# Branch products that wait for each head block, two gathered pairs added ahead of the sums, and one root per tile in the last norm

## What is computed

```python
for l in range(2):
    h = rms(x, norm1_g) * (1 + sc1) + sh1
    qa, ..., ga, gs, gr = split(h @ w_in)            # heads of three branches, three gates
    z = (sigmoid(ga) * (o_na @ w_br_na) + sigmoid(gs) * (o_swa @ w_br_swa)
         + sigmoid(gr) * (o_ret @ w_br_ret))         # the branch products
    x = x + g1 * (z @ w_out)
    h2 = rms(x, norm2_g) * (1 + sc2) + sh2
    x = x + g2 * experts(h2)                         # sum of each token's two expert rows
y = rms(x, final_norm_g)
# rms(x, g) = x * rsqrt(mean(x * x) + 1e-6) * g
```

## Time and profile before

| what | us |
|---|---|
| median of 3 timed runs | 1163.63 (1163.27 to 1164.51) |
| the profiled execution, its own time | 1159.58 |
| its span, from first to last instruction | 1157.8 |
| TensorE busy in the span | 1078.5 |
| VectorE busy | 689.8 |
| ScalarE busy | 440.6 |
| GpSimd busy | 197.0 |

### The profile page before, as it was taken

One profiled execution on the slowest core, in us unless ns is written; L12 is line 12 of the kernel. 1 busy time (PEld: TensorE's weight loads), 2 busy tenths in 40 slices (PEclk: granted clock), 3 DMA queues, 4 the chain that ended last, 5 costly groups with the idle time before them and its releaser, 6 DMA issues.

```text
span 1157.8 us, 23661 instructions
## 1 busy us (share of the span) xinstructions
PE 1078.5 (93%) x9845; PEld 895.0 (77%) x9845; DVE 689.8 (60%) x1477; ACT 440.6 (38%) x946; POOL 197.0 (17%) x224
## 2 busy tenths in 40 slices
PE   4999999999999989999879999999999998999995
PEld 2667778889897678888657677888998885888883
DVE  3535565645476657776663335655455858577667
ACT  4442245543423423332342232655234333333332
POOL 0021140000020123222211111300000301332313
PEclk9999999999999999999989999999999999999998
DMA  9988897223336699999846998421242467799985
GB/s 324 348 234 223 233 340 247 74 79 103 115 110 254 210 370 364 360 373 372 318 152 201 246 221 247 144 63 48 80 143 95 127 252 273 265 357 364 366 309 186
DMA packets 136335, 265.96 MB, mean 230 GB/s; under 512 B 9846, under 2 KB 91926, under 8 KB 128032
## 3 DMA queue, kind: packets, MB, share of 16 engines
q1 hardware_dynamic: 119280, 220.18, 55.6%
q0 software_dynamic: 16192, 42.06, 12.8%
q10 hardware_dynamic: 752, 2.15, 0.5%
HBM read 248.71 MB, written 26.74 MB: 238 GB/s over the span
## 4 chain that ended last, share of the span: by engine, by line
PE 78%; DVE 9%; DMA 6%; ACT 3%; issue 2%; POOL 1%; SPq 0%; DVEq 0%; POOLq 0%; ACTq 0%
PE ps L1036 17%; PE ps L827 16%; PE ps L1244 13%; PE ps L1285 6%; PE ps L1156 6%; PE ps L1171 5%; DMA arena<-in_ada_w 3%; PE ps L749 2%; DMA ring<-in_w_in 2%; PE ps L1234 2%; DMA arena<-scratch_xs,token_i 2%; PE ps L980 2%; PE ps L1020 2%; PE ps L1002 2%; PE ps L1323 1%
## 5 line engine op out<-in xcount | busy, mean ns | idle before, releaser
L627 DVE TENSOR_TENSOR w_lo<-ring,w_hi 128x512 fp32r<-128x512 f32 x128 | 87.7, 690 | 132.2 <-ACT w_hi L617 132.0
L617 ACT ACTIVATE w_hi<-ring 128x512 fp32r<-128x512 f32 x128 | 80.3, 631 | 209.8 <-PE ps L827 145.6
L624 DVE TENSOR_TENSOR w_lo<-ring,w_hi 128x512 fp32r<-128x512 f32 x128 | 88.1, 689 | 109.3 <-ACT w_hi L615 109.3
L1036 PE MATMUL ps<-h_hi,w_hi 128*128 128x384 f32 x384 | 133.8, 348 | 4.7 <-ACT arena L2452 4.7
L615 ACT ACTIVATE w_hi<-ring 128x512 fp32r<-128x512 f32 x128 | 80.3, 629 | 148.7 <-PE ps L1036 103.3
L1036 PE MATMUL ps<-h_hi,w_lo 128*128 128x384 f32 x384 | 128.7, 335 | 0.0
L1036 PE MATMUL ps<-h_lo,w_hi 128*128 128x384 f32 x384 | 128.7, 335 | 0.0
L827 PE MATMUL ps<-w_hi,h_hi 128*128 128x512 f32 x288 | 116.1, 403 | 5.0 <-issue 2.6
L827 PE MATMUL ps<-w_hi,h_lo 128*128 128x512 f32 x288 | 113.1, 393 | 0.0
L827 PE MATMUL ps<-w_lo,h_hi 128*128 128x512 f32 x288 | 113.0, 392 | 0.0
L1244 PEld LDWEIGHTS ps<-arena,ring 128*64 128x64 f32 x1920 | 80.2, 137 | 7.8 <-issue 7.8
(11 more groups left out here) (347 smaller groups left out, 2189.7 us busy)
## 6 DMA issues: line engine op xcount, KB each, us to landing
ring<-in_w_in SPq DMA_DIRECT2D x48, 1024.0 KB, 5.4
ring<-in_ada_w SPq DMA_DIRECT2D x34, 1024.0 KB, 9.8
ring<-in_w_down SPq DMA_DIRECT2D x18, 1024.0 KB, 12.6
ring<-in_w_up SPq DMA_DIRECT2D x16, 1024.0 KB, 11.2
ring<-in_w_gate SPq DMA_DIRECT2D x14, 1024.0 KB, 12.0
arena<-in_w_gate SPq DMA_DIRECT2D x10, 1024.0 KB
arena<-in_ada_w SPq DMA_DIRECT2D x8, 1024.0 KB, 10.9
ring<-in_w_out SPq DMA_DIRECT2D x8, 1024.0 KB, 5.1
```

The lines of the kernel that those rows point to most:

```text
L617: eng.activation(w_hi[:, q % 2], ring[:, slot, 2 * q:2 * q + 2, :], ACT.Copy).then_inc(whi_ready, 1)
L624: eng.tensor_tensor(gate_weights(w_lo, q), ring[:, SLOT[seg, l, c], k0:k0 + 4, j * P:(j + 1) * P], gate_weights(w_hi, q).bitcast(F32), ALU ...
L627: eng.tensor_tensor(w_lo[:, q % 2], ring[:, SLOT[seg, l, c], 2 * q:2 * q + 2, :], w_hi[:, q % 2].bitcast(F32), ALU.subtract).then_inc(wlo_ ...
L1036: mm = pe.matmul(ps[:, bank, 0:TOK], gate_weights(wx, q)[:, kk, :], hx[:, k, :], start=(k == 0 and n == 0), stop=(k == KT - 1 and n == 2))
```

## The change

Three edits, in the order of the diff:

1. In the first column of branch products PE waits for `o_lo` before each block k, for k + 1 low blocks, where it waited for four before the first and for eight before the fifth. The wait for the last gate still stands ahead of the fifth.
2. At the end of both layers DVE adds pairs 0 and 1 ahead of the first tile's sum, sums tiles 0 and 1, adds pair 2 and sums tile 2. In layer 0 that takes pair 1 from behind the first sum, and the two low quarters go from ahead of pair 2 to behind the last sum; in layer 1, the sum of tile 1 goes ahead of pair 2.
3. In the last norm POOL makes one root for each tile, and DVE's scaling of tile t waits for the root of tile t.

```diff
                     for h in range(2):
-                        if j == 0:
-                            pe.wait_ge(o_lo, l * KT + 4 * h + 4)
-                            if h == 1:
-                                pe.wait_ge(gate_ready, l * GT + GT)
+                        if j == 0 and h == 1:
+                            pe.wait_ge(gate_ready, l * GT + GT)
...
                         for kk in range(4):
                             k = 4 * h + kk
+                            if j == 0:
+                                pe.wait_ge(o_lo, l * KT + k + 1)
...
                 pair_summed(0)
-                if l + 1 == DEPTH:
-                    pair_summed(1)
+                pair_summed(1)
                 tile_summed(0)
+                tile_summed(1)
+                pair_summed(2)
+                tile_summed(2)
                 if l + 1 < DEPTH:
-                    pair_summed(1)
-                    tile_summed(1)
-                    dve.wait_ge(summed, l * TILES + TILES)
                     first_low_quarters(l + 1)
-                pair_summed(2)
-                if l + 1 == DEPTH:
-                    tile_summed(1)
-                tile_summed(2)
...
             for t in range(TILES):
-                dve.wait_ge(rstd_ready, DEPTH * RS + (2 if t == TILES - 1 else 1))
+                dve.wait_ge(rstd_ready, DEPTH * RS + t + 1)
...
-            def norm_roots(ready):
-
-                for t0, t1 in ((0, TILES - 1), (TILES - 1, TILES)):
+            def norm_roots(ready, parts=((0, TILES - 1), (TILES - 1, TILES))):
+
+                for t0, t1 in parts:
                     root((ssq_ready, ready + t1), ssq[:, t0:t1], msq[:, t0:t1], rstd[:, t0:t1], D, rstd_ready)
...
-            norm_roots(DEPTH * SSQ)
+            norm_roots(DEPTH * SSQ, [(t, t + 1) for t in range(TILES)])
```

## The result

| | before | after |
|---|---|---|
| median, range (5 runs each), us | 1163.27 (1158.09 to 1164.51) | 1152.86 (1149.47 to 1155.79) |
| ratio of the times, 95% interval | | 0.9914 [0.9892, 0.9936] |
| profiled execution: time, span, mean granted clock | 1159.58, 1157.8, .988 | 1152.86, 1151.0, .990 |

The two profiled executions stand 6.7 apart, close to the forecast, so one profile pair can't explain the result. Most of the experiments are about that gap.

The account below looks back on a forecast made before the run. PE was taken to bound the kernel, with 78% of the chain of waits. Terms of 5.0 (edit 1), 1.26 (edit 2) and 0.1 us (edit 3) sum to 6.4: 1163.63 - 6.4 = 1157.2, range 1155.0 to 1161.1.

Parts of the forecast that it names:

- edit 2's term: End of layer 0: pair 1's addition moves into DVE's idle time, so the copy and all behind come 1.26 us earlier.
- a clock term: Branch start: after a shorter idle PE stays at full clock, gaining 1.34 us in each layer, bounds 0 and 1.37.
- the 1.41: Branch start: PE waits for one low block of DVE instead of four, gaining 1.41 us in each layer.
- The 0.25 for an exposed weight load: Branch start: 0.25 us taken off each layer's gain for a weight load or two that close waits can't hide.
- nothing by itself: End of layer 1: edit 2 moves only the sum of tile 1, by 1.2 us, with no gain by itself.
- The 1.43 and 0.72: Last norm: a POOL power takes 0.72 us alone but 1.43 beside DVE's scaling, limiting edit 3's gain to 0.1.
- its bounds (-0.6 to 1.2): Last norm: edit 3 gains 0.1 us, 1.2 with no hindrance, -0.6 if both steps of root 2 wait for scalings.
- The loads follow: Loads at layer 0's end and in the projection move up with PE; the rival, that they don't: 1161.0, chance 0.11.
- the clock did not fall at the branches: Rival at the branch starts: the clock falls as before, total gain 4.2 us, time 1159.4, chance 0.20.
- the gate is not the releaser: Rival at the branch start: the last gate frees PE, leaving 1.36 us of gain, time 1162.3, chance 0.06.
- the projection is not bound by its loads: Rival in layer 1's projection: loads land later, eight chunks stall by about 1.3 us each, time 1167.6, chance 0.05.
- the way to the median and the range: The 6.4 us gain taken from the timed median 1163.63; range 1155.0 to 1161.1, using a run spread of 1.2.

Follow-up runs that it names:

- the copy: The kernel before, unchanged, run as a kernel of its own for a second profile and more timed runs: 1164.01 us, ratio 1.0011.
- the filled kernels: Before and after, each with dummy matmuls in PE's idle time at the same five places, waits left: 1155.83 us and 1153.03 us.
- root_only: The kernel before with the third edit alone: 1165.50 us, ratio 1.0013.
- before_warm: The kernel before with three dummy matmuls of 128x512 ahead of the branch products in both layers, no wait changed: 1159.29 us, ratio 0.9951.
- branch_only: The kernel before with the first edit alone, in two sets on different chips: 1154.85 us (ratio 0.9914), then 1158.57 us (ratio 0.9956).
- branch_first: The kernel before with the first edit in layer 0 alone: 1161.21 us, ratio 0.9985.
- branch_second: The kernel before with the first edit in layer 1 alone: 1160.36 us, ratio 0.9964.
- pairs_only: The kernel before with the second edit alone: 1159.55 us, ratio 0.9966.
- branch_pairs: The kernel before with the first and second edits together, the last norm's roots as before: 1156.18 us, ratio 0.9938.
- tile_one_last: The kernel after with the last norm's scalings in the order of tiles 0, 2, 1: 1155.01 us in one run.
- before_seam_warm: The kernel before with dummy matmuls only around the end of layer 0 and the start of layer 1's projection: 1158.91 us, ratio 0.9972.
- all_warm: Dummy matmuls at five idle places of PE, put into before (1155.83 us, ratio 0.9941) and into after (1153.03 us, ratio 0.9914).
- after_again: The kernel after, unchanged, run as a kernel of its own for a second profile and more timed runs: 1157.09 us, ratio 0.9941.

## Why the prediction was right and wrong

All runs together give the best size: 115 timed runs of before in the four later jobs (12 of them of the copy) have a mean of 1163.0 and a median of 1163.2; the 23 of after in three jobs have 1154.5 and 1155.1. That is 8.1 to 8.5 us, ± 0.7. Each job by itself gives 9.4, 6.2 and 10.5, weighted by their errors 7.7 ± 0.7. **The change gives about 8 us, not 10.4, and rather more than 6.4.** So 1 to 2 us of the miss are the prediction's, and the rest is the scatter of five runs.

How much of it is clock can be estimated from the granted clock of each run. A stretch at half clock loses half its length, so a run loses its span times (1 - mean clock), if PE is busy in its low stretches. (At the end of the program it isn't, but that is alike in both.) This gives 17.2 us in the 115 runs of before and 12.2 in the 23 of after. By this estimate 5.0 ± 0.7 us of the gain are clock and 3.5 ± 0.4 everything else, the shorter waits in the main; the filled kernels stood 3.4 ± 1.0 apart. The rows below price 4.8 and 4.5.

**Step that failed first: edit 2's term.** "the four matmuls (5.96 us, rows 7) and all behind move up: gain 1.26 us" priced the moved addition and nothing of the clock, though the prediction gave edit 1 a clock term. The 5.96 was a sign: at full clock these eight rows take 3.60. Profiles of kernels with and without edit 2 (those with dummies at this place left out), with the time from the first row of line 772 to the end of layer 1's first chunk:

| kernels | idle of PE ahead of line 772 | 772 to the end of the first chunk |
|---|---|---|
| without edit 2: before twice, `root_only`, `before_warm`, `branch_only` twice, `branch_first`, `branch_second` | 3.64 to 3.65 | 20.8 to 21.9, mean 21.4 |
| with it: after three times, `pairs_only`, `branch_pairs`, `tile_one_last` | 2.25 or 2.26, once 1.63 | 17.6 to 22.0, mean 19.5 |
| filled with dummies: `before_seam_warm`, both `all_warm` | 0 to 0.4 | 17.3 to 17.5 |

Without edit 2 the eight rows and the first chunk were both slowed in all eight; with it the chunk was at full clock in two of six, and the eight rows in three. That is 1.4 us of wait and 1.8 ± 0.6 of clock, 3.2 in place of 1.26, and `pairs_only` measured 3.8 ± 0.9 against its own job and 2.9 against all runs of before. Of the 1.8, 1.2 lie in the eight rows right behind the shorter wait, 5.7 us in the mean without the edit and 4.5 with it. The 0.6 in the chunk is less sure: PE's idle time ahead of it is 2.59 or 2.60 us with and without the edit, and two of six against none of eight can be chance. What the low clock costs in this piece is shown apart from the edit: the dummies of `before_seam_warm` leave the waits and bring it from 21.4 to 17.5.

**Edit 1 was right in mechanism and nearly in size.** The wait goes by DVE's first block, as worked out: idle 1.35 us (forecast 1.31), 1.36 gained of the 1.41. The clock stayed: each of 12 branch starts behind an idle of 2.71 took 9.91 to 10.17 us for its 48 matmuls, and each of 16 behind 1.35 took 8.56 to 8.59. One row of a like idle time was all that the prediction had for that, and all 16 bore it out. That is 10.07 - 8.58 = 1.49 for each layer, where 1.34 was forecast. The 0.25 for an exposed weight load was wrong: PE is busy for all of the 3.40 us behind the start, and its 48 matmuls take 8.58. So 2 x (1.36 + 1.49) = 5.7 against 5.0; the two sets of runs, 17 in all, have a mean of 1157.3, 5.7 under all of before. The first 8.7 did not come back in the second set (5.2 ± 0.9) nor in the two layers apart (4.5 ± 1.5), and no row prices it. But all three against the before of their own jobs, weighted, give 6.7 ± 0.6, and the first set's mean clock was higher by .005 where the second's was by .0025. So a part of the clock that the rows don't price isn't excluded.

**Edit 3: the mechanism right, the credit wrong.** POOL's root of the last tile is held by DVE's scaling, with a gap ahead of the last one, as said. But the held instruction is the product (1.30 us), not the power (0.55), and the gain of 0.44 belongs to edit 2, whose part in layer 1 the prediction called "nothing by itself". (The 1.43 and 0.72 that the prediction set side by side were of a 128x1 and of a 128x2 power; a 128x1 power beside nothing takes 0.55 to 0.57.) Edit 3 alone costs 0.36 in its profile, within its bounds (-0.6 to 1.2).

The rows sum up to 5.7 + 3.2 + 0.4 = 9.3, the runs to 7.7 to 8.5 with a standard error of 0.7. **The loads follow**, as counted: the load at the end of layer 0 (18.54 at 549.66 in rows 9) and that of the projection (10.18 at 632.09 in rows 10) became

```profile
548.06 18.97 DMA arena<-in_ada_w
...
627.96 10.31 DMA ring<-in_w_in
```

They land 1.2 and 4.0 us sooner.

No rival came about: the clock did not fall at the branches, the gate is not the releaser, and the projection is not bound by its loads. Its fifth chunk waits for one as before (PE idle for 1.44 us, 1.30 before), the chunks behind it for none.

**Step that failed second: the way to the median and the range.** "since the timed runs spread by 1.2" took the spread of three runs for that of the kernel. Its standard deviation is 2.8 us over 115 runs, from 1156.5 to 1171.4. Medians of five drawn from the 23 runs of after lie between 1152.9 and 1157.1 in 8 draws of 10, and under 1155.0, the range's low end, in more than 3 of 10. Which side of it the five runs fell was in part luck. The size forecast plus what was missed, 1155.1, is in the range given; the median of the five runs is not. Subtracting 6.4 from 1163.63 was sound in itself, since that median was near the 1163.2 of the many runs; the profile of before (1159.58) was the one far off: only 18 of the 115 runs are as short.

What stays open: why an execution has more low stretches or fewer. Two jobs had after 9.4 and 10.5 below before in the means and one 6.2. The later jobs were on different chips, and no run tells the chip from chance. At the first scores of layer 1, over 100 us behind the end of layer 0, the clock fell in seven of the ten profiles that lack edit 1 or edit 2 and have no dummy there, and in none of the five that have both; at the same place in layer 0, ahead of the edits, in four and three. Whether the edits act that far on stays open.

## What to carry to other kernels

Where PE resumes behind an idle time, compare its first matmuls with the same ones elsewhere: eight rows that take 5.96 us in place of 3.60 are part of what a shorter wait may give back, at every place that an edit touches and not only at the first. A single profile of a kernel with many such places is one draw: take the spread from many runs before a range is set, and look for the same place in two or three profiles before a low stretch is charged to an edit. Before a root is split to start sooner on POOL, see what DVE runs beside it.

## What the runs showed of the hardware

- The granted clock fell behind each of the 12 idle times of 2.71 us at the branches and behind none of the 16 of 1.35. In three of the 12 the first matmul still took 0.41 us, as at full clock, and the fall came just behind it. The length of the last idle time doesn't settle it: behind the 2.59 or 2.60 us ahead of layer 1's first chunk that chunk was slowed in 12 of 14 profiles, behind 2.05 us in that projection (`branch_only`) it stayed, with the chunk in 8.40. Ahead of the first scores of each layer PE is idle for 1.44 or 1.45 and then 0.93 or 0.94 us in every profile, and there the clock fell in 7 of the 15 profiles that have no dummy there, in layer 0 and again in layer 1. One of these, layer 0 in `after_again`:

```profile
163.00:166.00 3.00, 3.00 (x17) 2.46 (x18) 1.25 (x6) 1.65 (x8) 3.00 (x7) 0.50 1.02 389
```

- The time of a run goes with its mean clock: of the 115 runs of before, the 29 with .983 or less have a mean of 1165.2, the 67 between 1163.0, and the 19 with .988 or more 1159.7.
- One POOL instruction on 128x1 values takes 0.19 us with DVE idle and 1.23 to 1.30 beside a DVE scaling with two inputs in SBUF, a tile and the gains, and ends within 0.1 us behind it.
